# Three boundaries between residual stages: the second norm's squares from sums gathered for the first, one pass over the K-tiles, and h's low parts on GpSimd

## The reference

```python
mods = (silu(c) @ w_ada + b_ada)            # shifts sh, scales sc and gates gt
h = rmsnorm(x, g_pre[0]) * (1 + sc1) + sh1
x = x + 0.5 * gt1 * rmsnorm(swiglu(h, w_gu1, w_dn1), g_post[0])
h = rmsnorm(x, g_pre[1]) * (1 + sc2) + sh2
y = token_mixer(h, ...)
x = x + gt2 * rmsnorm(y, g_post[1])
h = rmsnorm(x, g_pre[2]) * (1 + sc3) + sh3
x = x + 0.5 * gt3 * rmsnorm(swiglu(h, w_gu2, w_dn2), g_post[2])

def rmsnorm(x, g):
    return x * rsqrt(mean(x * x, axis=-1) + 1e-6) * g
```

## Time and profile before

| what | value |
|---|---|
| device time, three runs | 2735.16, 2738.63 and 2740.59 us; median 2738.63 |
| the profiled execution | 2737.11 us, span 2735.3 us, mean granted clock of PE 0.978 |
| busy in the span | PE 97%, DVE 42%, ACT 37%, POOL 38% |

### The profile page before, as it was taken

How to read it: one execution, slowest core, us unless ns; L and a number is a source line. 1 busy time by engine, 2 the same in 40 slices (tenths; PEclk the granted TensorE clock), 3 DMA queues, 4 the chain that set the end, 5 groups by cost and what they waited for, 6 DMA issues and landing times.

```text
span 2735.3 us, 36041 instructions
## 1 busy us (share of the span) xinstructions
PE 2642.1 (97%) x12940; PEld 2145.9 (78%) x12940; DVE 1156.3 (42%) x2091; ACT 1001.9 (37%) x1604; POOL 1037.2 (38%) x442
## 2 busy tenths in 40 slices
PE   6999999999999999999999999999999999999998
PEld 4788888777777688888888888889665667888887
DVE  6544226674444124644315543222444455422212
...
GB/s 257 211 196 184 138 128 32 55 73 75 84 82 80 85 97 134 117 196 196 174 123 67 195 193 137 108 111 89 40 46 56 79 78 90 86 99 97 95 108 93
DMA packets 78570, 313.31 MB, mean 115 GB/s; under 512 B 9072, under 2 KB 11888, under 8 KB 69008
## 3 DMA queue, kind: packets, MB, share of 16 engines
...
...
## 4 chain that ended last, share of the span: by engine, by line
PE 85%; DVE 7%; issue 5%; ACT 3%; POOL 0%; DMA 0%; DVEq 0%; ACTq 0%; POOLq 0%
PE bank L1737 23%; PE bank L1739 23%; PE bank L1738 22%; PE bank L1778 2%; PE bank L1779 2%; PE bank L1780 2%; PE pair L1948 1%; PE pair L2014 1%; PE bank L2024 1%; PE bank L2032 1%; PE bank L2169 1%; DVE h_lo L1172 1%; DVE lev L1397 1%; DVE lev L1396 1%; PE bank L2153 1%
## 5 line engine op out<-in xcount | busy, mean ns | idle before, releaser
L536 POOL TENSOR_TENSOR w_lo<-raw,w_hi 128x1024 fp32r<-128x1024 f32 x414 | 1019.3, 2464 | 1645.2 <-ACT w_hi L580 1584.6
L580 ACT ACTIVATE w_hi<-raw 128x1024 fp32r<-128x1024 f32 x420 | 444.1, 1059 | 1118.7 <-PE bank L1739 1095.6
L1737 PE MATMUL bank<-h_hi,w_hi 128*128 128x512 f32 x2064 | 834.3, 404 | 4.8 <-POOL w_lo L536 3.6
L1739 PE MATMUL bank<-h_hi,w_lo 128*128 128x512 f32 x2064 | 807.6, 391 | 0.0
L1738 PE MATMUL bank<-h_lo,w_hi 128*128 128x512 f32 x2064 | 806.5, 391 | 0.0
L1737 PEld LDWEIGHTS bank<-h_hi,w_hi 128*128 128x128 f32 x2064 | 390.4, 189 | 98.0 <-issue 17.3
L1739 PEld LDWEIGHTS bank<-h_hi,w_lo 128*128 128x128 f32 x2064 | 388.9, 188 | 83.2
L1738 PEld LDWEIGHTS bank<-h_lo,w_hi 128*128 128x128 f32 x2064 | 389.8, 189 | 77.8 <-issue 4.1
L1737 PE MATMUL bank<-act_hi,w_hi 128*128 128x512 f32 x616 | 239.6, 389 | 0.0
L1738 PE MATMUL bank<-act_lo,w_hi 128*128 128x512 f32 x616 | 239.6, 389 | 0.0
L1739 PE MATMUL bank<-act_hi,w_lo 128*128 128x512 f32 x616 | 239.6, 389 | 0.0
...
## 6 DMA issues: line engine op xcount, KB each, us to landing
...
```

Of the source, the lines that this page charges most:

```text
L536: nc.gpsimd.tensor_tensor(wl[s][:], raw[s][:], wh[s][:], ALU.subtract).then_inc(lo_done, 1)
L580: nc.scalar.activation(wh[s][:], raw[s][:], ACT.Copy).then_inc(hi_done, 1)
L1737: MM(out, wh[s][:, k], a, start=first and j == 0, stop=False)
L1739: ins = MM(out, wl[s][:, k], a, start=False, stop=end and j == len(tiles) - 1)
```

## The change

At the three boundaries with a norm on either side, the sum of squares of the new x is no longer taken from the new x. With r the first norm's factor of a token and p the product of gate and gain, the new x is x + r p y, and its sum of squares is the old one plus r times (the sum of 2 p y x plus r times the sum of p p y y). So DVE gathers three sums while the output tiles come: `ssacc` (y y), `yyacc` (p p y y) and `xyacc` (2 p y x). The old sum of squares is kept per token in `sx`. `new_sum` works the new one out on small columns, and both norms' factors come from one reduction over partitions. DVE then goes over the K-tiles once per half (`norms`): scratch, x, and x times gain times the second factor into `xr`. ACT adds the shift twice, once rounding into `hh` and once in place into `xr`, and POOL makes `hl` by subtracting (`h_low`). In PE's list the sums are placed later in the second half of the last output tile, there are six single-column matmuls for a half instead of four and eight (b = 1, 3) or six and eight (b = 2), the second half's slab 2 is interleaved with slabs 0 and 1, and the logits of the mixer's head come inside slab 3. The first stage additionally copies the sums of squares of the input x with one ACT instruction and four matmuls.

```diff
-            def sum_squares(b, half):
-
-                hc, done = halves(half), 8 * (b - 1) + 4 * half
-                for n in range(KT - 3):
-                    pool.wait_ge(sx_done, 8 + 16 * (b - 1) + 8 * half + n + 1)
-                    if n:
-                        if n > 1:
-                            pool.wait_ge(sx_added, done + n - 1)
-                        nc.gpsimd.tensor_tensor(y[:, n, hc], y[:, n, hc], y[:, n - 1, hc], ALU.add).then_inc(sx_added, 1)
+            def h_low(p, half):
+
+                hc, done = halves(half), 16 * p + 8 * half
+                for n in range(KT):
+                    pool.wait_ge(hh_done, done + n + 1)
+                    nc.gpsimd.tensor_tensor(hl[:, n, hc], xr[:, n, hc], hh[:, n, hc], ALU.subtract).then_inc(h_done, 1)
...
+                    shift = mod[:, b, 24 * v + n:24 * v + n + 1]
+                    ins = nc.scalar.activation(hh[:, n, hc], xr[:, n, hc] if TWO[p] else scratch(n), ACT.Identity, bias=shift)
+                    if TWO[p]:
+                        ins = nc.scalar.activation(xr[:, n, hc], xr[:, n, hc], ACT.Identity, bias=shift)
+                    ins.then_inc(hh_done, 1)
...
-                        nc.scalar.activation(y[:, t], src, ACT.Identity, scale=post_g[:, t:t + 1]).then_inc(acc_free[(m + t) % 2], 1)
+                        else:
+                            act.wait_ge(ssadd, SSADD[b] + t - 1)
+                        nc.scalar.activation(y[:, t], src, ACT.Identity, scale=post_g[:, t:t + 1])
+                        nc.scalar.activation(squared(t) if t else ssacc[:], src, ACT.Square).then_inc(sq_done, 1)
...
-                    nc.scalar.activation(sq[:, t % 2, hc], src, ACT.Square).then_inc(sqh_done, 1)
+                    src = bk[:, halves(t - t0)]
+                    act.wait_ge(ssadd, SSADD[b] + t - 1)
+                    nc.scalar.activation(y[:, t, hc], src, ACT.Identity, scale=post_g[:, t:t + 1])
+                    nc.scalar.activation(squared(t, half)[:, hc], src, ACT.Square).then_inc(sqh_done, 1)
...
-            def new_squares(b, half, tiles=range(KT)):
-
-                for n in tiles:
-                    act.wait_ge(x_done, 16 * (b - 1) + 8 * half + n + 1)
-                    nc.scalar.activation(y[:, n, halves(half)], x[:, n, halves(half)], ACT.Square).then_inc(sx_done, 1)
-
...
-                if TWO[b]:
-                    now = KT if per > 1 else 5
-                    new_squares(b, 0, range(now))
+                    std_new(b, 0)
                     if per == 1:
                         out_halves(b, c, m, 1)
-                        new_squares(b, 0, range(now, KT))
-                    std(ev + 1, 4)
+                    split_h(b, 0, range(0, 2))
                     if per > 1:
                         out_halves(b, c, m, 1)
-                    split_h(b, 0, range(0, 3))
-                    std(ev + 2, 2)
-                    split_h(b, 0, range(3, 5))
+                    split_h(b, 0, range(2, 4))
                     high(c + 3)
-                    split_h(b, 0, range(5, KT))
-                    new_squares(b, 1)
-                    std(ev + 3, 6, sums=SC1)
+                    std(b, 1)
+                    split_h(b, 0, range(4, 6))
+                    split_h(b, 0, range(6, KT))
+                    std_new(b, 1)
                     table(func)
                     split_h(b, 1)
+                    if b > 1:
+                        high(c + 4)
...
+                    if not n and (f or c + 4 >= AHEAD + len(ONCE)) and (z or not TWO[stage_of("ffn", f)]):
                         high(c + 4)
...
+                V.tensor_copy(sums[:, 0:4], sums_at(half)[:, 2:6])
+                recip(ev, c0)
+                dve.wait_ge(rcol_done, ev + 1)
+                for t in range(2):
+                    ins = V.tensor_scalar(rcol[:, 4 + c0 + t:5 + c0 + t], sums[:, t:t + 1], rcol[:, c0 + t:c0 + t + 1], sums[:, 2 + t:3 + t],
+                                          ALU.mult, ALU.add)
+                chain.link(ins)
+                for t in range(2):
+                    ins = V.tensor_scalar(sx[:, c0 + t:c0 + t + 1], rcol[:, 4 + c0 + t:5 + c0 + t], rcol[:, c0 + t:c0 + t + 1],
+                                          sx[:, c0 + t:c0 + t + 1], ALU.mult, ALU.add)
+                chain.link(ins)
+                V.tensor_scalar(sx[:, c0:c0 + 2], sx[:, c0:c0 + 2], 0.0, None, ALU.max).then_inc(sx_set, 1)
...
+            def norms(b, half, among):
                 for pair in range(0, KT, 2):
                     for n in (pair, pair + 1):
                         if pair:
                             dve.wait_ge(x_done, done + n - 1)
-                        scaled(n)
+                        V.tensor_tensor(scratch(n), y[:, n, hc], rows[:, 0:HALF], ALU.mult).then_inc(y_done, 1)
+                    if pair == 0:
+                        recip(ev + 1, 4 + 2 * half)
                     for n in (pair, pair + 1):
                         dve.wait_ge(y_done, done + n + 1)
                         V.tensor_tensor(x[:, n, hc], x[:, n, hc], scratch(n), ALU.add).then_inc(x_done, 1)
+                    if pair == 0:
+                        dve.wait_ge(rstd_done, ev + 2)
+                    for n in (pair, pair + 1):
+                        dve.wait_ge(x_done, done + n + 1)
+                        V.scalar_tensor_tensor(xr[:, n, hc], x[:, n, hc], pre_a[:, n:n + 1], rows[:, HALF:T], ALU.mult, ALU.mult)\
+                            .then_inc(u_done, 1)
+                    if pair in among:
+                        among[pair]()
...
+                    chain.link(V.tensor_scalar(post_x[:], post_g[:], 2.0, None, ALU.mult))
+                    V.tensor_tensor(post_s[:], post_g[:], post_g[:], ALU.mult).then_inc(post_ready, 1)
...
+                        else:
+                            dve.wait_ge(ssadd, SSADD[b] + t)
+                            V.scalar_tensor_tensor(ST[:], acc[(m + t) % 2][:], post_x[:, t:t + 1], x[:, t], ALU.mult, ALU.mult)\
+                                .then_inc(acc_free[(m + t) % 2], 1)
+                            V.tensor_tensor(ssacc[:], ssacc[:], squared(t), ALU.add)
+                            V.scalar_tensor_tensor(yyacc[:], squared(t), post_s[:, t:t + 1], yyacc[:], ALU.mult, ALU.add)
+                            tile_evacuated(dve, m + t)
+                            V.tensor_tensor(xyacc[:], xyacc[:], ST[:], ALU.add).then_inc(ssadd, 1)
...
+            def half_sums(b, m, half):
...
+                for t in range(t0, KT):
+                    product = V.scalar_tensor_tensor(ST[:, hc], bk[:, halves(t - t0)], post_x[:, t:t + 1], x[:, t, hc], ALU.mult, ALU.mult)
+                    if t == KT - 1:
+                        product.then_inc(acc_free[q % 2], 1)
+                    else:
+                        chain.link(product)
+                    V.tensor_tensor(ssacc[:, hc], ssacc[:, hc], squared(t, half)[:, hc], ALU.add)
+                    V.scalar_tensor_tensor(yyacc[:, hc], squared(t, half)[:, hc], post_s[:, t:t + 1], yyacc[:, hc], ALU.mult, ALU.add)
+                    if t == KT - 1:
+                        tile_evacuated(dve, q)
+                    last = V.tensor_tensor(xyacc[:, hc], xyacc[:, hc], ST[:, hc], ALU.add)
...
-                    recip(ev, 0)
-                    post(b, m, 0, ev, SC1)
-                    recip(ev + 1, 4)
-                    norm_h(b, 0, ev + 1, SC1, lambda: recip(ev + 2, 2))
-                    post(b, m, 1, ev + 2, ST)
-                    recip(ev + 3, 6)
-                    norm_h(b, 1, ev + 3, ST)
+                    if b == 1:
+                        dve.wait_ge(x_sum, 2)
+                        chain.link(V.tensor_copy(sx[:], TP[:, 0:TT]))
+                    half_sums(b, m, 0)
+                    new_sum(b, 0)
+                    norms(b, 0, {2: lambda: half_sums(b, m, 1), 4: lambda: new_sum(b, 1)})
+                    norms(b, 1, {})
...
+                if TWO[b]:
+                    pe.wait_ge(half_summed, 2 * (b - 1) + half + 1)
+                    for q, a in enumerate((ssacc, yyacc, xyacc)):
+                        for t in range(2):
+                            ins = MM(sums_at(half)[:, 2 * q + t:2 * q + t + 1], a[:, t0 + P * t:t0 + P * (t + 1)], ones[:, 0:1],
+                                     start=True, stop=True)
+                    ins.then_inc(s_sum, 1)
+                    return
...
-            def sum_new(b, half):
-
-                t0, src = HALF * half, range(KT - 4, KT)
-                pe.wait_ge(sx_added, 8 * (b - 1) + 4 * (half + 1))
-                for n in src:
...
-                                if half and done == (2 if TWO[b] else 6):
+                                if half and done == (8 + 5 * (SPLIT[b] - 1) if TWO[b] else 6):
                                     sum_out(b, 0)
-                                if half and done == (4 if TWO[b] else 9):
-                                    spread(ev, 0, SC1)
```

(18 more changed lines are left out.)

191 lines of the change are left out of this document (102 added, 89 removed).

## The result

The changed kernel takes 2722.01 us (median of four runs, 2721.06 to 2722.57) against 2739.61 of the kernel before (four runs, 2735.16 to 2741.19): 17.6 us less, ratio 0.9944 with the 95% interval 0.993 to 0.9958. Forecast were 2718.8 and 19.8 us less. 2722.01 lies at the upper edge of the forecast's own range (2714.5 to 2722) and nearer to the clock rival's 2724.

What follows compares the result with a forecast made beforehand. PE, busy 97% of the span, was taken as the bound. Terms 8.3 + 4.9 + 8.5 - 0.9 - 1.0 = 19.8 us less gave 2717.3, plus 1.5 for the median 2718.8 us; own range 2714.5 to 2722, overall 2710 to 2731.

Steps and rivals of the forecast that it cites:

- the clock rival: Heads of all three boundaries: PE's clock falls to half, 5.5 us lost, 2724 us; chance 0.20.
- Until the first h: First boundary: sums at +2.9, spreads +5.3 and +7.9, first K-tile of h +10.75 instead of +14.1; second boundary's about +12.2.
- The pace: First half's joint slabs: DVE sets the speed, 2.1 us a pair of K-tiles, 1.05 each, against PE's 0.72.
- Collisions: Second half's sums with two SBUF inputs wait for POOL, 0.5 us each: 1.0, 2.0 and 1.0 at the three boundaries.
- First boundary: Last half output tile through the head: 47.3 to 39.7 us, 7.7 less; 8.3 with the chain into the mixer.
- Second boundary: Two halved output tiles through the head: 45.0 us instead of 49.8, 4.9 less, slow clock left in.
- Third boundary: Last half output tile through the head: 7.7 us less, 8.5 with the 0.73 wait behind it gone.
- Elsewhere: Input: four summing matmuls cost PE 0.9 us; output tiles: added ACT and DVE work hidden, PE's banks free in time.
- 1.0 for the clock: Boundaries 1 and 3: four chances in ten each of losing 1.3 us to a slower PE clock.
- The output tiles' rival: Six output tiles at the second boundary: DVE's new sums become the bound, 26 us lost, 2745 us; chance 0.04.
- that of the slower chain: DVE over ACT to POOL: POOL holds DVE's passes, 1.8 us a K-tile, 19.5 us over forecast, 2738; chance 0.04.
- a clock of 1.00 in the first and third joint slabs: Joint slabs of boundaries 1 and 3: PE's clock stays at 1.00, listed among what would show the forecast right.

Runs made afterwards that it cites:

- The delayed factor: Changed kernel with the second factor's spread at boundaries 1 and 3 behind the last output tile instead of its 17th triple: 2723.1 us, ratio 0.995.
- Scratch in SBUF: Changed kernel with the product of y and first factor written to SBUF instead of a PSUM bank, so x plus product has two SBUF inputs: 2724.1 us, 0.9947.

## Why the prediction was right, point by point

- **Until the first h.** Sums, spreads and first h at the first and third boundaries came within 0.1 us of the forecast; at the second +12.07 against +12.2. At the first and third boundaries the later first factor cost PE nothing: it has no wait ahead of the first h. The second reduction's place ahead of the pass made the first h 3.3 us earlier there. The delayed factor shows what this moment is worth: 1.8 us of delay made the third head 1.3 longer, at a better clock. How the rest of a head's gain divides between the single pass, the low parts on POOL and the interleaved slab 2 (0.7 to 1.9 us by its undoing) was not measured piece by piece.
- **The pace.** 2.11 us a pair with DVE behind it, as worked out from the earlier trace rows.
- **Collisions, 4.0 us counted.** One operation of eight took 0.5 longer, the only one that started behind an operation of POOL under way (1086.65, at the second boundary). At four POOL ran nothing, at three POOL started second and took 0.83 to 0.96 instead of 0.74. Scratch in SBUF shows that DVE does wait where it comes second. So the mechanism was right, and the term should have been near its lower bound.
- **Waits of DVE, nothing counted.** At the first boundary 0.8 for the sums, 1.4 and 2.25 for the spreads. The second half's h was complete at +34.0 and not at +31.3. The two errors nearly cancel at the end of the head: slabs 0 to 2 of the second half ended at +37.4, forecast 36.8.
- **First boundary, 8.3 counted, 5.9 and 7.1 measured.** This is the term that was too large. ACT's chain into the mixer was named as what sets the end, and then sized after PE's gain. It gained 6.3. PE's further gain turned into a wait of 1.4, or was used up by the clock's fall at the logits. (The logits stand behind three K-tiles of slab 3, not two as the prediction has it.)
- **Second boundary, 4.9 counted, 6.0 measured.** The 1.1 us are there at the end of the joint slabs already (+26.2, forecast +27.3). Of 2.0 counted there for collisions 0.5 came. The clock was as slow as before, 13.7 us at half in either kernel, as forecast.
- **Third boundary, 8.5 counted, 7.5 measured.** The 0.73 behind it went as foreseen; the clock was at half for 6.8 us in the joint slabs (0.92 over the head), where half a microsecond had been set aside.
- **Elsewhere.** The input's four sums cost PE what was counted:

```profile
280.80 1.05 PE L1966 MATMUL bank<-ones,sq 1*128 1x1 f32 x8
```

The output tiles' operations took 0.76, 0.68, 0.74 and 0.68, 2.86 a tile, beside a bank freed in time, with one exception. In the mixer ACT came late to the second output tile, since it had waited for a slab's transfer, and PE waited for that bank two tiles on:

```profile
1050.90 0.50 PE L1806 MATMUL bank<-oa_hi,w_hi 128*128 128x512 f32 x1 [0.49 <-DVE bank L1258]
```

ACT at the first boundary's end, to be held against the earlier trace rows. It takes up the next slab 47.0 us behind the half tile's start, 52.9 before:

```profile
434.43 0.67 ACT L760 ACTIVATE lax<-pair,cols 128x512 f32<-128x512 f32 x1
...
441.58 1.06 ACT L585 ACTIVATE w_hi<-raw 128x1024 fp32r<-128x1024 f32 x1 [1.48 <-PE bank L1846]
```

- **The sum.** The three heads gave 19.5 against 21.7 counted, less 1.0 for the clock. The first FFN was 1.4 us shorter in the profile instead of 0.9 longer, and mixer and rest 2.2 and 2.8 longer, with the clock at half for 4.3 and 7.0 us more. Run once more, the first FFN was 1.2 us longer than before, so its 1.4 us are luck. 19.5 + 1.4 - 2.2 - 2.8 is 15.9, the spans differ by 16.1 and the medians by 17.6. That the total is near the forecast owes something to this spread: the medians of the later rounds put it at 14.9.
- **The rivals.** The output tiles' rival and that of the slower chain did not come; both of their mechanisms are real, and when provoked cost 0.6 us and up to 1.7 us a head. The clock's rival came in part: in the first profile it fell in head 1 twice, in the joint slabs and at the logits, and in head 3 once. The prediction had named a clock of 1.00 in the first and third joint slabs as a sign, and this sign failed; run once more, head 1 had 1.00 throughout and head 3 had the same fall.
